# A fused two-block transformer kernel on one core: ScalarE's exponentials placed ahead of a pair's outputs in three attentions, VectorE's low part of the outputs a step later

## The reference, cut to what matters

```python
# moba (8 heads), swa (16 heads, window 128, a sink), fox (16 heads, forget gates)
s = q @ k.T + bias                      # 256 x 256 per head, masked to the causal part
p = softmax(s)                          # swa: the sink adds exp(sink - m) to the sum
o = p @ v                               # 256 x 64 per head
y = o.reshape(256, heads * 64) @ w_out
```

## Time and profile before

| | us |
|---|---|
| median of 3 runs | 1482.85 (1481.79 to 1484.59) |
| the profiled execution | 1480.96 |
| its span, first to last instruction | 1479.2 |
| TensorE busy | 1403.3 (95%) |
| VectorE busy | 1083.6 (73%) |
| ScalarE busy | 720.6 (49%) |
| mean granted TensorE clock | 0.987 |

### The profile page before, as it was taken

The page is one execution under the profiler, slowest core; times in us unless marked ns, Lnnn a source line. Parts: engine busy times, 40 slices in busy tenths (PEclk is TensorE's granted clock), DMA queues, the critical chain, the costliest instruction groups (busy, mean ns, idle before and its releaser), DMA issues.

```text
span 1479.2 us, 18509 instructions
## 1 busy us (share of the span) xinstructions
PE 1403.3 (95%) x7259; PEld 1162.8 (79%) x7259; DVE 1083.6 (73%) x1508; ACT 720.6 (49%) x1011; POOL 145.1 (10%) x215
## 2 busy tenths in 40 slices
PE   2899999999999999999999999999999999899998
PEld 1688988999878888775688887788878766688886
DVE  5778976999878997756678887787787445566444
ACT  3554455444554343765643336534457555553332
POOL 1111000111012220001011110111110100000000
PEclk9899999999999999999999999999999999999999
DMA  9777655889669997450588986788854521475552
GB/s 352 270 218 253 218 196 191 302 276 308 205 218 352 341 349 252 138 171 1 173 300 301 300 295 222 243 310 301 293 190 140 189 74 59 141 256 188 181 185 73
DMA packets 189289, 333.63 MB, mean 226 GB/s; under 512 B 8850, under 2 KB 132478, under 8 KB 188180
## 3 DMA queue, kind: packets, MB, share of 16 engines
q1 hardware_dynamic: 161392, 236.02, 47.5%
q0 software_dynamic: 27232, 96.21, 19.2%
q10 hardware_dynamic: 580, 0.23, 0.1%
HBM read 331.27 MB, written 1.15 MB: 225 GB/s over the span
## 4 chain that ended last, share of the span: by engine, by line
PE 84%; DVE 7%; ACT 4%; issue 2%; DMA 2%; SPq 0%; ACTq 0%; DVEq 0%
PE bank L1517 10%; PE bank L1519 10%; PE bank L1518 10%; PE bank L1480 8%; PE bank L1482 7%; PE bank L1481 7%; PE bank L1412 4%; PE bank L1413 4%; PE bank L1414 4%; PE bank L1648 3%; DVE lo L989 3%; PE bank L1650 3%; PE bank L1649 3%; PE bank L1724 1%; DMA V<-in_ada_w 1%
## 5 line engine op out<-in xcount | busy, mean ns | idle before, releaser
L989 DVE TENSOR_TENSOR lo<-raw,hi 128x2048 fp32r<-128x2048 f32 x215 | 491.0, 2287 | 88.2 <-ACT hi L554 87.2
L554 ACT ACTIVATE hi<-raw 128x2048 fp32r<-128x2048 f32 x215 | 405.6, 1910 | 17.8 <-DMA raw<-in_w_out 12.7
L1517 PE MATMUL bank<-hi,h_hi 128*128 128x512 f32 x704 | 278.1, 395 | 3.6 <-DVE lo L989 1.9
L1519 PE MATMUL bank<-hi,h_lo 128*128 128x512 f32 x704 | 274.6, 390 | 0.0
L1518 PE MATMUL bank<-lo,h_hi 128*128 128x512 f32 x704 | 274.2, 389 | 0.0
L1480 PE MATMUL bank<-hi,o_hi 128*128 128x512 f32 x504 | 204.6, 406 | 11.0 <-DVE lo L989 9.0
L1482 PE MATMUL bank<-hi,o_lo 128*128 128x512 f32 x504 | 197.7, 392 | 0.0
L1481 PE MATMUL bank<-lo,o_hi 128*128 128x512 f32 x504 | 197.2, 391 | 0.0
L666 ACT ACTIVATE KT<-bank 128x256 f32<-128x256 f32 x88 | 33.8, 384 | 313.8 <-PE bank L1519 313.7
L1517 PEld LDWEIGHTS bank<-hi,h_hi 128*128 128x128 f32 x704 | 132.2, 188 | 33.5 <-DVE lo L989 3.9
L1519 PEld LDWEIGHTS bank<-hi,h_lo 128*128 128x128 f32 x704 | 132.1, 188 | 28.2
(11 more groups left out here) (214 smaller groups left out, 1989.7 us busy)
## 6 DMA issues: line engine op xcount, KB each, us to landing
raw<-in_ffn_w SPq DMA_DIRECT2D x176, 512.0 KB, 5.2
ada<-in_ada_w POOLq DMA_DIRECT2D x100, 512.0 KB, 6.0
raw<-in_ffn_w SPq DMA_DIRECT2D x44, 1024.0 KB, 6.0
V<-in_ada_w POOLq DMA_DIRECT2D x76, 512.0 KB, 5.9
raw<-in_w_up SPq DMA_DIRECT2D x22, 1024.0 KB, 5.7
raw<-in_w_in SPq DMA_DIRECT2D x16, 1024.0 KB, 7.8
raw<-in_fox_w_in SPq DMA_DIRECT2D x12, 1024.0 KB, 5.1
raw<-in_w_down SPq DMA_DIRECT2D x11, 1024.0 KB, 5.2
```

The lines of the kernel that those rows point to most:

```text
L554: nc.scalar.activation(hi[:, n % NS, :], raw[:, n % NS, :], ACT.Copy).then_inc(hi_ready, 1)
L989: nc.vector.tensor_tensor(lo[:, n % NS, :], raw[:, n % NS, :], hi[:, n % NS, :].bitcast(F32), ALU.subtract).then_inc(lo_ready, 1)
L1517: mm(bank[:, :], xk_hi, wh[:, i, :], start=k == 0, stop=False, skip_group_check=True)
L1519: ins = mm(bank[:, :], xk_lo, wh[:, i, :], start=False, stop=k == KD - 1, skip_group_check=True)
```

## The change

`attention_step` of ScalarE becomes `attention_exps` and `attention_outs`: the exponentials come first, then (in swa's step 2 and fox's steps 1 to 6 after the block work of the step) the copy of the turned probabilities, then the pair's high part. VectorE's low part of a pair's outputs goes from even step t to step t + 1, between the maximum and the scaling; the last pair's stays at the last step. In fox the high part of unit 16 goes from step 14 to 15 and its low part from step 14 to 17. In the prologue, unit 1 is split on ScalarE between the two halves of `modulated(0, 0)` and on VectorE before the second half of `split_h(0, 0)`.

```diff
--- before.py
+++ after.py
@@ -582,8 +582,8 @@
                     nc.scalar.activation(xn(t, h), x[:, t, 512 * h:512 * (h + 1)], ACT.Copy,
                                          scale=rms[:, t, 4:5]).then_inc(xn_ready, 1)
 
-            def modulated(b, t):
-                for h in range(2):
+            def modulated(b, t, halves=(0, 1)):
+                for h in halves:
                     act.wait_ge(acol_ready, 2 * b + h + 1)
                     n = 4 * b + 2 * t + h
                     act.wait_ge(xt_done, n + 1)
@@ -747,14 +747,16 @@
                 act.wait_ge(pv_done, 2 * n + 2)
                 nc.scalar.activation(o_hi[:, pair, :], value_bank(2 * pair), ACT.Copy).then_inc(ohi_done, 1)
 
-            def attention_step(s, t):
+            def attention_exps(s, t):
+                if t < HEADS[KINDS[s]]:
+                    exps(s, t)
+
+            def attention_outs(s, t):
                 nh = HEADS[KINDS[s]]
+                if 0 <= t - 2 < nh:
+                    pt_copy(s, t - 2)
                 if 0 <= t - 3 < nh and (t - 3) % 2:
                     out_hi(s, (t - 3) // 2)
-                if t < nh:
-                    exps(s, t)
-                if 0 <= t - 2 < nh:
-                    pt_copy(s, t - 2)
 
 
             act.wait_ge(c_turned, 1)
@@ -788,8 +790,9 @@
                 ins = nc.scalar.activation(table_rows[0:heads, n, :], G[n][0:heads, 0:384], ACT.Copy)
             ins.then_inc(bias_rows, 1)
             split_to(0)
-            modulated(0, 0)
+            modulated(0, 0, (0,))
             split_to(1)
+            modulated(0, 0, (1,))
             modulated(0, 1)
             act.wait_ge(small_full, SMALL_LOADED)
             nc.scalar.activation(f_hi[:, 0:KD, :], f_w[:, :, :], ACT.Copy).then_inc(f_hi_done, 1)
@@ -826,7 +829,8 @@
                     block_values(s, 1)
                     split_through(s, 8)
                     for t in range(HEADS[kind] + 3):
-                        attention_step(s, t)
+                        attention_exps(s, t)
+                        attention_outs(s, t)
                         if t in (2, 4):
                             i = (t - 2) // 2
                             act.wait_ge(unit_done, base + 7 + i)
@@ -871,10 +875,11 @@
                     split_through(s, 6)
                     block_square(s, 4)
                     for t in range(HEADS[kind] + 3):
-                        attention_step(s, t)
+                        attention_exps(s, t)
                         if t == 2:
                             block_square(s, 5)
-                        elif t == 3:
+                        attention_outs(s, t)
+                        if t == 3:
                             block_roots(s, 4)
                         elif t in (5, 6):
                             block_evict(s, t - 1)
@@ -908,19 +913,20 @@
                     block_values(s, 1)
                     split_through(s, 8)
                     for t in range(HEADS[kind] + 3):
-                        attention_step(s, t)
+                        attention_exps(s, t)
                         if 1 <= t < 5:
                             block_square(s, t + 3)
                         if 3 <= t < 7:
                             block_evict(s, t + 1)
+                        attention_outs(s, t)
                         if t in (2, 4):
                             block_roots(s, t + 2)
                         if t in (5, 8):
                             block_values(s, 2 + t // 8)
                         if t in (0, 1):
                             split_through(s, 9 + t)
-                        elif t in (3, 7, 8, 10, 12, 14):
-                            split_through(s, 11 + (3, 7, 8, 10, 12, 14).index(t))
+                        elif t in (3, 7, 8, 10, 12, 15):
+                            split_through(s, 11 + (3, 7, 8, 10, 12, 15).index(t))
                         elif t == 17:
                             split_through(s, 17)
                     split_through(s, NUNITS[kind] + 1)
@@ -1152,10 +1158,13 @@
                 nh = HEADS[kind]
                 if t < nh:
                     max_of(s, t)
+
+                if t >= 5 and t % 2:
+                    out_lo(s, (t - 5) // 2)
                 if 0 <= t - 1 < nh:
                     normalise(s, t - 1)
-                if 0 <= t - 3 < nh and (t - 3) % 2:
-                    out_lo(s, (t - 3) // 2)
+                if t == nh + 2:
+                    out_lo(s, nh // 2 - 1)
 
             def step(ins):
 
@@ -1272,8 +1281,8 @@
             split_to(0)
             split_h(0, 0, (0,))
             pro_columns(1)
+            split_to(1)
             split_h(0, 0, (1,))
-            split_to(1)
             split_h(0, 1)
             for s, kind in enumerate(KINDS):
                 base = W0[s]
@@ -1391,8 +1400,8 @@
                             block_sums(s, t + 3)
                         if t < 4:
                             split_through(s, 8 + t)
-                        elif t in (8, 9, 11, 13, 14):
-                            split_through(s, 12 + (8, 9, 11, 13, 14).index(t))
+                        elif t in (8, 9, 11, 13, 17):
+                            split_through(s, 12 + (8, 9, 11, 13, 17).index(t))
                         if t in (2, 4):
                             block_norm(s, t + 2)
                             block_norm(s, t + 3)
```

## The result

The changed kernel takes 1457.55 us (median of 4 runs, 1455.82 to 1458.54), the kernel before 1482.34 beside it (4 runs, 1481.79 to 1484.59): ratio 0.9829, interval 0.9812 to 0.9846. Forecast were 1462 and a gain of 21; the gain is 24.8. The profiled execution took 1455.82 (span 1454.0), which against that of before is 25.14 less. Lines behind L750 have numbers up to 9 higher in the changed file: the turn L1706 is L1715, the values L1724 and L1726 are L1733 and L1735, swa's logits L1687 are L1696, the block turn L1662 is L1671, a low part L989 is L995 and out_lo L1147 is L1153; in an experiment's file they lie between.

The account below looks back on a forecast made before the run. TensorE, busy 95% of the span, bounds the kernel; only its idle time and low clock can be won. Swa 7.4 + fox 14.2 + moba 0 + prologue 0.4 = 22.0, less 1: 21 off 1482.85, 1462; own range 1458 to 1466, wider 1457 to 1473.

Parts of the forecast that it names:

- swa: forecast 7.4: Second attention: 3.4 at the start, 1.5 at steps 9 and 10, 1.0 at step 13, 1.5 at steps 15 to 17.
- fox: forecast 14.2: Third attention: 3.15 us to logits 8, then 1.6, 2.55, 0.3, 3.9 and 2.7 from there to its tail.
- 1.6 + 2.55 + 0.3: Fox: low clock behind logits 8 gone, 1.6; waits and low clock at steps 9 and 10, 2.55; step 13, 0.3.
- 3.9 + 2.7: Fox: step 16's 3.80 us turn wait gone by moving unit 16's split, 3.9; the tail from turn 14 on, 2.7.
- the 0.4 of the values for out_lo: Expected sign: a new wait of about 0.4 us of the values for out_lo near each attention's end.
- a sign of being wrong: TensorE waiting over 1 us for out_lo, low stretches without a gap before them, or a later stage longer by the attention's loss.
- Rival A: In swa and fox all four low-clock stretches stay, 7.2 us not won: gain 15, 1468; chance 0.16.
- The 1 us that I took off: Discount on the summed gain of 22.0, because two of the low stretches may stay in part.
- Prologue: forecast 0.4: First block's norm 1.15 us sooner, a 2.4 us gap perhaps with low clock behind it; bounds -1.2 and +0.4, -0.4 taken.
- B: VectorE's scaling behind out_lo delays odd-step turns, 0.75 us for each of 14 pairs, 10.5 off the gain: 1472; chance 0.12.
- C: No change, 1483: the named waits are not binding and others (norms, logits) end at the same time; chance 0.05.
- D: Slower, 1490: out_lo behind a low part and the maximum holds the value bank in ten steps, 30 us lost; chance 0.05.

Follow-up runs that it names:

- Experiments 3: The change without the prologue's edit and without moving fox's unit 16 split, only the two attention orders, against the kernel before: 1461.78 us, ratio 0.987.
- 4: The changed kernel with fox's unit 16 split put back to step 14 on both engines: 1459.12 us, ratio 0.9849 to the kernel before.
- Experiments 1: The kernel before with only fox's unit 16 split moved, high part to step 15 and low part to step 17: 1474.44 us, ratio 0.9953.
- 9: The kernel before with swa's three filler products of step 5 issued at the end of step 4: 1480.29 us, ratio 0.9994.
- 2: The kernel before with only the prologue's edit, unit 1's split moved forward on both engines: 1480.09 us, ratio 0.9993.
- 6: The kernel before with only VectorE's low part of the outputs a step later: 1480.61 us, ratio 1.0001.
- 5: The kernel before with only ScalarE's attention order changed (exponentials, copy, high part of the outputs): 1471.79 us, ratio 0.9935.
- 12: The changed kernel with both fox's unit 16 high part at step 16 and moba's first two block norms sooner: 1456.99 us, ratio 0.984 to the kernel before.
- 10: The changed kernel with fox's high part of unit 16 moved from step 15 to 16: 1456.7 us, ratio 0.9837 to the kernel before.
- 11: The changed kernel with moba's first two block norms ahead of low parts in the prologue: 1456.42 us, ratio 0.9835 to the kernel before.

## Why the prediction was right and where it was not

The direction and the mechanism were right, and step by step most of the sizes; the total was 4 us short. In the profiled pair the miss is 25.1 - 21 = 4.1: 3.1 of it are two low stretches outside the places of the sum, 1.0 is what I took off for stretches that might stay.

**swa: forecast 7.4, measured 7.5.** Here is the changed kernel's ScalarE at the start of the stretch; the steps answer to the earlier trace rows:

```profile
658.97 0.31 ACT L699 ACTIVATE hstd<-hstd,eps 128x16 f32<-128x16 f32 x1
659.30 1.28 ACT L730 ACT_TABLE_LOAD   x1
660.59 0.41 ACT L730 ACTIVATE work<-work,stat 128x129 f32<-128x129 f32 x1
...
661.49 0.47 ACT L742 ACTIVATE work<-bank 128x384 f32<-128x384 f32 x1
661.86 0.36 ACT L748 ACTIVATE o_hi<-bank 128x256 fp32r<-128x256 f32 x1
```

The table load follows the roots at once instead of waiting for the pair's product, and the copy stands ahead of out_hi. It starts at 661.49; my 664.0 for its end is 661.96 when the 2.0 us are taken off by which the whole stretch begins sooner, and it ends at 661.96. TensorE's turn has no wait any more (a bracket at the end of its row would tell of one), and the next logits come 2.7 us behind it, where it took 4.04 in the earlier trace rows and I had put 2.6:

```profile
662.18 0.55 PE L1715 MATMUL bank<-ident,work 128*128 128x128 f32 x3
...
664.87 0.48 PE L1696 MATMUL bank<-KT,QT 64*128 64x128 f32 x2
```

The first exponential starts 1.29 us after its table load does (660.59 - 659.30), as in the earlier trace rows. The Trainium skill's drain of 1.38 us ("ScalarE: Activation LUTs", "What ACT_TABLE_LOAD costs") is not in this trace either, and swa's gain is the one without it.

**fox: forecast 14.2, measured 13.8.** To 1213.9: 3.15 against 3.3. From there to 1256.6: 1.6 + 2.55 + 0.3 = 4.45 against 4.2. The tail: 3.9 + 2.7 = 6.6 against 6.3. The new wait of 0.8 at the last turn came as described. Of the 0.4 of the values for out_lo near each attention's end, fox has 0.2 and swa none (its 0.5 is for the copy). An out product also waits 1.02 for the last out_lo, just over the mark that I had set as a sign of being wrong, but the kernel before has the same wait of 1.02 there, so it tells nothing against the walk. The changed kernel's fox, last steps, all engines:

```profile
1237.62 1.90 ACT L554 ACTIVATE hi<-raw 128x2048 fp32r<-128x2048 f32 x1
1239.43 0.48 ACT L742 ACTIVATE work<-bank 128x384 f32<-128x384 f32 x1
...
1240.05 0.52 PE L1715 MATMUL bank<-ident,work 128*128 128x128 f32 x3 [0.78 <-ACT work L742]
1240.21 0.42 DVE L1153 TENSOR_TENSOR o_lo<-bank,o_hi 128x256 fp32r<-128x256 f32 x1 [4.11 <-ACT o_hi L748]
1240.56 2.28 DVE L995 TENSOR_TENSOR lo<-raw,hi 128x2048 fp32r<-128x2048 f32 x1
1240.78 0.62 PE L1733 MATMUL bank<-work,V 128*64 128x256 f32 x2 [0.21 <-DVE o_lo L1153]
```

The moved high part holds the copy up for 0.78 us, and the low part (1240.56) stands where it delays nothing. But the sum held while one attribution in it fell. I gave 3.9 of step 16 to the moved split as if the orders left that gap as it was. Experiments 3 and 4 show that the orders alone take the 3.8 gap away and put one of 2.3 for out_lo in its place: the whole tail's worth of the moved split is 6.3 without them and 2.1 to 3.2 beside them. The prediction walked each step with all edits in and so found the right end, but it could not have said what either edit was worth.

**Low clock inside the attentions: right.** Rival A (it stays, 1468) fell: four stretches of four are gone. Experiments 1 and 9 show the link by itself, since in each one gap was removed or halved and, of the stretches in the attentions, only the one behind it went. Where the gap was left, the stretch stood every time: the one at 666 in five executions of five (both of the kernel before, experiments 1, 2 and 6), one in fox's tail in six of six (both, experiments 2, 5, 6 and 9). But a gap of the same size doesn't always bring one: behind 2.3 us there is one in experiment 3 and none in 4. The Trainium skill, page "TensorE: Matmul & The Clock Gate", section "What's actually happening", has the gate follow how busy TensorE has lately been; the four stretches bear it out, while the one at 1164.8, below, has no idle time ahead of it and is not explained by idle time. A low stretch without a gap before it was also one of my signs of being wrong; none of the named ones is, but this one is. The 1 us that I took off for stretches that may stay was not due.

**Prologue: forecast 0.4, measured 1.2.** The first product's second half came sooner and the gap of 2.4 us at the block's norm came as described. I took -0.4, a value between full clock behind it (-1.2) and low (+0.4); in both traces of the change it was the one, in experiment 2 the other. It is one or the other by execution, not a value between. Of the 1.2 only 0.5 shows in the profiled pair, because at 36 us the changed kernel stood 0.7 later.

**Not in the forecast: 3.1 us, most of the miss.** The step that failed is the term put at nothing: outside the named places the sum leaves the time as it was (moba zero, the shift kept behind each attention), since the low stretches in it are those of the earlier trace rows alone. The kernel before has three more in mid-run, at 144.3, 222.8 and 1164.8. The one at 222.8, behind a wait of 2.22 us for a low part of the activations, stands in the changed kernel too (at 220.5) and in every execution profiled, so it costs both alike:

```profile
222.80:226.20 3.40, 3.40 (x18) 0.50 0.00 0
```

The other two are gone in the change. TensorE in the kernel before, and below it the same multiplications in the changed one (a row's two lengths are the gain):

```profile
143.06:147.70 4.64, 4.64 (x26) 0.63 0.90 305
1160.90:1168.31 7.41, 7.41 (x25) 0.77 0.65 239
```

```profile
142.57:145.73 3.16, 3.15 (x26) 1.00 0.93 298
1151.16:1156.99 5.83, 5.83 (x24) 1.00 0.83 306
```

The order there is the same in both, and so is what stands ahead: at 143.06 a wait of 2.30 for a low part (2.29 after), and ahead of 1164.8 no idle time at all, only the small products of the first logits, which begin at 1160.90. Each costs 1.5 to 1.6 us.

Over the fourteen executions profiled the stretch at 144 stands in seven. Six of them are among the seven with the old prologue (before, 1, 3, 5, 6, 9; the kernel before's second execution lacks it), and these six have the one at 48.7 as well; of the seven with the new prologue only one has it (12, at 140.6), and experiment 2, the prologue's edit alone, doesn't, and gains 1.5 there. The one at 1165 stands in all seven executions that lack either of the two orders (both of the kernel before, 1, 2, 5, 6 and 9), and in four of the seven with both (4, 10, 11 and 12, at 1154 to 1156; not in 3 nor in either execution of the change). So both are rarer with the edits in, while the one at 144 also came and stayed away in one and the same kernel. Whether the shift of the work ahead makes them rarer, so that this part of the gain is the change's own, or the counts are chance, is left open.

That may also be why the medians give less than the pair of profiles: against the 46 runs of the kernel before in the experiments (medians 1480.7 to 1481.1) the change is 23 to 24 us faster, and the sum of my places measured, 0.5 + 7.5 + 13.8 = 21.8, stands against 22.0 before the discount.

**The other rivals.** B (1472) did not come: the one turn that still waits does so for the copy, behind the moved high part, and not for the scaling. C was refuted. D (1490) did not come as a whole, but its mechanism is real: in fox it takes back what VectorE's order alone might give (3.5 us for out_lo; in swa it is the copy's wait that stays), it is the 2.3 of experiments 3 and 4, and the moved split is what keeps it to 0.2. I had taken it for a risk in ten steps; in these traces it took hold where a unit's low part was queued just ahead of an odd step's maximum and had itself to wait long for its high part (5.24 us in experiment 3), which was so at one step of fox. That this is the condition is my reading of one place; no run varied it elsewhere.

## What to carry to other kernels

Where two engines both queue work behind the same product (here out_hi on ScalarE and out_lo on VectorE), try the two moves together before either is dropped: one alone gave 8.9, the other 0, both 19.3. Judge what an edit is worth by adding it to the kernel before and by taking it out of the final one; the moved split gave 6.3 by the one and 2.1 by the other. List every low-clock stretch of the trace before, also those that no edit touches: each that may or may not come is 1.5 us on the range, and a second profile of the same kernel shows which ones come and go.

## What the runs showed of the hardware

The same multiplications behind the same gap of 2.3 us ran at 1.2 GHz in one execution of the kernel before and at 2.4 GHz in its second (143 us), while those behind 2.2 us at 222 were at 1.2 GHz in all fourteen executions, and a stretch at 1.2 GHz also followed multiplications without any idle time between them (1164.8, behind the small logits products; the rows of 143.06 and 1160.90 above). The same stretch differed in length too (6.8 us at 1260.6 in the kernel before, 10.2 at 1257.5 in its second execution), and one of 3.4 cost 1.5 to 1.6 us against the same work at full clock. ScalarE's move to its exponentials took the table load of 1.28 us and nothing more that the trace shows. The kernel before spread over 7.9 us in 46 runs (1476.8 to 1484.6), the changed one over 2.7 in 5 (1455.8 to 1458.5), experiment 5 over 10.8 in 10; so few runs of the change don't show that its spread is smaller.
